# Splitting the weights of the head loops on ACT and DVE in a two-layer recurrent decoder step

## What is computed

```python
def _hgrn_mixer(h, w_in, lb, out_norm, w_out, S0):
    proj = h @ w_in
    q, fz, i, g = jnp.split(proj, [HGRN_F, 2 * HGRN_F, 2 * HGRN_F + D_MODEL], axis=-1)
    ...
    o, S = _hgrn_recurrence(q, k, v, log_f, S0.astype(F32))
    o = _rmsnorm(o, out_norm) * jax.nn.silu(g...)
    return o.reshape(B, T, D_MODEL).astype(h.dtype) @ w_out, S

def _trunk(x, ...):
    for i in range(DEPTH):
        h = _rmsnorm(x, norm_mix[i])
        y, S = _hgrn_mixer(h, ...) if i % N_MIXERS == 0 else _gdn_mixer(h, ...)
        x = x + y
        u = _rmsnorm(x, norm_mlp[i]) @ mlp_w_up[i]
        x = x + jnp.square(jax.nn.relu(u)) @ mlp_w_down[i]
```

## Time and profile before

| | |
|---|---|
| three runs | 2123.45, 2127.5, 2131.67 us; median 2127.5 us |
| span of the profiled execution (first to last instruction) | 2127.4 us |
| PE busy | 1885.8 us (89%) |
| DVE busy | 1200.8 us (56%) |
| POOL busy | 776.9 us (37%) |
| ACT busy | 449.8 us (21%) |
| mean granted clock of PE | 0.898 |

### The profile page before, as it was taken

One profiled execution on the slowest core, in us unless ns is written; L12 is line 12 of the kernel. 1 busy time (PEld: TensorE's weight loads), 2 busy tenths in 40 slices (PEclk: granted clock), 3 DMA queues, 4 the chain that ended last, 5 costly groups with the idle time before them and its releaser, 6 DMA issues.

```text
span 2127.4 us, 34241 instructions
## 1 busy us (share of the span) xinstructions
PE 1885.8 (89%) x13227; PEld 1784.2 (84%) x13227; DVE 1200.8 (56%) x1818; ACT 449.8 (21%) x899; POOL 776.9 (37%) x423
## 2 busy tenths in 40 slices
PE   4798888888999999996789889889878899999997
PEld 3788888887999999996678778778767899999996
DVE  5777777785744242575455555465561573516163
ACT  1323322331100000012233233233341110000011
POOL 1422222222566555563121211121210365656562
PEclk9988888888999999998789888888885999999998
DMA  5122221221233322231111211211100123322331
GB/s 161 50 61 60 60 59 52 60 61 42 83 87 90 90 78 84 79 81 52 40 31 43 52 30 41 52 30 41 52 21 21 55 86 90 89 82 87 89 89 42
DMA packets 257434, 135.99 MB, mean 64 GB/s; under 512 B 6698, under 2 KB 255876, under 8 KB 257348
## 3 DMA queue, kind: packets, MB, share of 16 engines
q1 hardware_dynamic: 219700, 114.03, 18.8%
q10 hardware_dynamic: 37648, 20.68, 3.3%
HBM read 122.70 MB, written 12.00 MB: 63 GB/s over the span
## 4 chain that ended last, share of the span: by engine, by line
PE 42%; DVE 6%; ACT 3%; issue 2%; POOL 0%; DVEq 0%; ACTq 0%; POOLq 0%
PE pj L449 27%; PE rr L487 2%; PE rr L699 2%; PE rr L723 2%; DVE pr L1532 1%; PE rr L470 1%; PE rr L715 1%; PE rr L792 1%; PE rr L708 1%; DVE ws L1603 1%; PE rr L780 1%; PE rr L644 1%; DVE ol L1742 1%; ACT ws L1028 1%; PE rr L798 1%
## 5 line engine op out<-in xcount | busy, mean ns | idle before, releaser
L416 POOL TENSOR_SCALAR w_hi<-w_raw 128x1024 fp32r<-128x1024 f32 x209 | 223.5, 1069 | 1299.5 <-PE pj L449 1268.8
L418 POOL TENSOR_TENSOR w_lo<-w_raw,w_hi 128x1024 fp32r<-128x1024 f32 x209 | 553.0, 2646 | 17.5
L449 PE MATMUL pj<-xh,w_hi 128*128 128x272 f32 x2064 | 480.2, 316 | 19.4 <-DVE xl L1298 10.0
L449 PE MATMUL pj<-xh,w_lo 128*128 128x272 f32 x2064 | 453.2, 303 | 0.0
L449 PE MATMUL pj<-xl,w_hi 128*128 128x272 f32 x2064 | 452.7, 303 | 0.0
L449 PEld LDWEIGHTS pj<-xh,w_hi 128*128 128x128 f32 x2064 | 348.9, 204 | 48.7 <-issue 30.2
L449 PEld LDWEIGHTS pj<-xl,w_hi 128*128 128x128 f32 x2064 | 350.9, 204 | 0.0
L449 PEld LDWEIGHTS pj<-xh,w_lo 128*128 128x128 f32 x2064 | 350.1, 204 | 0.0
L449 PE MATMUL pj<-oh,w_hi 128*128 128x272 f32 x1280 | 271.2, 293 | 16.7 <-DVE ol L1322 5.4
L449 PE MATMUL pj<-oh,w_lo 128*128 128x272 f32 x1280 | 268.3, 292 | 0.0
L449 PE MATMUL pj<-ol,w_hi 128*128 128x272 f32 x1280 | 267.2, 291 | 0.0
(11 more groups left out here) (275 smaller groups left out, 2290.0 us busy)
## 6 DMA issues: line engine op xcount, KB each, us to landing
w_raw<-in_mlp_w_up_dram SPq DMA_DIRECT2D x64, 512.0 KB, 4.0
w_raw<-in_mlp_w_down_dram SPq DMA_DIRECT2D x64, 512.0 KB, 3.7
w_raw<-in_hgrn_w_in_dram SPq DMA_DIRECT2D x32, 512.0 KB, 4.0
w_raw<-in_gdn_w_in_dram SPq DMA_DIRECT2D x32, 512.0 KB, 4.1
out_dram<-S ACTq DMA_DIRECT2D x16, 512.0 KB, 3.3
S<-in_state_hgrn_dram ACTq DMA_DIRECT2D x8, 512.0 KB, 4.0
w_raw<-in_hgrn_w_out_dram SPq DMA_DIRECT2D x8, 512.0 KB, 3.7
S<-in_state_gdn_dram ACTq DMA_DIRECT2D x8, 512.0 KB, 4.1
```

The lines of the kernel that those rows point to most:

```text
L416: nc.gpsimd.tensor_scalar(w_hi[:, s], w_raw[:, j], 1.0, 1.0, ALU.mult, ALU.mult).then_inc(w_split, 1)
L418: nc.gpsimd.tensor_tensor(w_lo[:, s], w_raw[:, j], w_hi[:, s], ALU.subtract).then_inc(w_split, 1)
L449: last = mm(pj[:, s, b, 0:HALF], w[:, s, k, :], v[:, k, b * HALF:(b + 1) * HALF], start=(k == 0 and a == 0), stop=(k == KT - 1 and a == 2))
```

## The change

Units 4 to U_HOUT + 1 and U_GIN + 4 to U_GOUT + 1, thirty in each layer, are no longer split by POOL. ACT makes the high part (`high`, an activation of kind Copy) and DVE the low part (`low`, a subtraction), at places written by hand into the programs of the heads. POOL keeps the first units of each layer and the MLPs. One semaphore becomes four, and whoever waits for a low part asks the semaphore of the engine that makes it (`low_part`). In SP's loads the first two heads and the output projections are unrolled, so that each knows its semaphore; the transfers and their order stay. In the diff below `run` (a loop over POOL's units) and the unrolled loads are left out.

```diff
-        w_split = sem("weights_split")
+        hi_act = sem("high_parts_by_scalar")
+        hi_pool = sem("high_parts_by_gpsimd")
+        lo_dve = sem("low_parts_by_vector")
+        lo_pool = sem("low_parts_by_gpsimd")
...
+        def on_gpsimd(u):
+
+            return u < 4 or U_HOUT + 2 <= u < U_GIN + 4 or u >= U_GOUT + 2
+
+        POOL_UNITS = [u for u in range(U_END) if on_gpsimd(u)]
+        DVE_UNITS = [u for u in range(U_END) if not on_gpsimd(u)]
+
+        def split_count(u):
+
+            part = POOL_UNITS if on_gpsimd(u) else DVE_UNITS
+            return part.index(u) + 1
+
+        def low_part(r, u):
+
+            at = r + u if isinstance(r, int) else u + (8 if u < U_HOUT - RAW or U_GIN - RAW <= u < U_GOUT - RAW else 0)
+            return (lo_pool if on_gpsimd(at) else lo_dve), split_count(at) - (at - u) + r
+
+        def raw_count(u):
+
+            return 16 * (u // RAW + 1) + (16 if u >= U_AB and u % RAW == U_AB % RAW else 0)
...
-                    free = fixed(sp, r * 2 + (2 * (U + j) - 6))
+                    done, n = low_part(r, U + j - RAW)
+                    free = fixed(sp, n)
                     sp.wait_ge(x_in[0], 16)
-                    sp.wait_ge(w_split, free)
+                    sp.wait_ge(done, free)
...
-            def split(n, j, extra=0):
-                u, s = n * 4 + j, j % SPLIT
-                loaded, free = fixed(pool, n * 16 + (16 + extra)), fixed(pool, u - 1)
+            def split(r, u):
+
+                j, s = u % RAW, u % SPLIT
+                at = r + u if isinstance(r, int) else u + 4
+                count = split_count(at) - (at - u) + r
+                loaded, free = fixed(pool, r * 4 + raw_count(at) - 4 * (at - u)), fixed(pool, r + u - 1)
+                written = fixed(pool, count)
                 pool.wait_ge(ones_set, 1)
                 pool.wait_ge(w_in[j], loaded)
-                if not (isinstance(n, int) and u < SPLIT):
+                if not (isinstance(r, int) and r + u < SPLIT):
                     pool.wait_ge(w_used, free)
-                nc.gpsimd.tensor_scalar(w_hi[:, s], w_raw[:, j], 1.0, 1.0, ALU.mult, ALU.mult).then_inc(w_split, 1)
-                pool.wait_ge(w_split, u * 2 + 1)
-                nc.gpsimd.tensor_tensor(w_lo[:, s], w_raw[:, j], w_hi[:, s], ALU.subtract).then_inc(w_split, 1)
-
-            for j in range(RAW):
-                split(0, j)
-            with pool.Fori(1, U_AB // 4) as n:
-                for j in range(RAW):
-                    split(n, j)
-
-            ab = U_AB % RAW
-            with pool.Fori(U_AB // 4, U_END // 4) as n:
-                for j in range(RAW):
-                    split(n, j, 16 if j == ab else 0)
-            for j in range(U_END % 4):
-                split(U_END // 4, j, 16 if j == ab else 0)
+                nc.gpsimd.tensor_scalar(w_hi[:, s], w_raw[:, j], 1.0, 1.0, ALU.mult, ALU.mult).then_inc(hi_pool, 1)
+                pool.wait_ge(hi_pool, written)
+                nc.gpsimd.tensor_tensor(w_lo[:, s], w_raw[:, j], w_hi[:, s], ALU.subtract).then_inc(lo_pool, 1)
...
+            for u in range(4):
+                split(0, u)
+            run(U_HOUT + 2, U_AB)
+            for u in range(U_AB, U_GIN + 4):
+                split(0, u)
+            run(U_GOUT + 2, U_END)
...
-                    pe.wait_ge(w_split, u * 2 + 2)
+                    pe.wait_ge(*low_part(r, U + j))
...
+            def high(h, u):
+
+                j, s = u % RAW, u % SPLIT
+                loaded, free = fixed(act, h * 16 + raw_count(u)), fixed(act, h * 4 + (u - 1))
+                act.wait_ge(w_in[j], loaded)
+                act.wait_ge(w_used, free)
+                f(w_hi[:, s], w_raw[:, j], ACT.Copy).then_inc(hi_act, 1)
...
                         hgrn_prepare(n, nxt)
+                        if m == 4:
+                            high(nxt, 2)
+                        if m == 32:
+                            high(nxt, 3)
                 if nxt is not None:
                     hgrn_prepare(7, nxt)
+                    high(nxt, 4)
...
                 s.did(f(oh[:, ds(h, 1)].rearrange("p o n -> p (o n)"), oo, ACT.Copy), "hi")
                 if nxt is not None:
+                    high(nxt, 5)
...
+            def gdn_head(h, prev, nxt, final=False):
 
                 v, s, t = st["gr"]
                 X, Tt, VN, oo, sqr = (gd[n] for n in ("X", "Tt", "VN", "oo", "sq"))
+                if nxt is not None:
+                    high(nxt, U_GIN + 3)
...
                         gdn_prepare(f"L{n}", nxt)
+                        if m == 16:
+                            high(nxt, U_GIN + 4)
...
                         gdn_prepare(f"C{c}", nxt)
+                        if c == 0:
+                            high(nxt, U_GIN + 5)
+                        if c == NC - 1 and not final:
+                            high(nxt, U_GIN + 6)
...
             for slot in range(3, 10):
                 hgrn_prepare(slot, 0)
+            high(0, 4)
+            high(0, 5)
...
                 gdn_prepare(slot, 0)
+            high(0, U_GIN + 4)
+            high(0, U_GIN + 5)
             gdn_first_inverse(0)
+            high(0, U_GIN + 6)
...
+            def low(h, u):
+
+                written = fixed(dve, h * 4 + (split_count(u + 4) - 4))
+                dve.wait_ge(hi_act, written)
+                tt(w_lo[:, u % SPLIT], w_raw[:, u % RAW], w_hi[:, u % SPLIT], ALU.subtract).then_inc(lo_dve, 1)
...
                         hgrn_prepare(n, nxt)
+                        if m == 8:
+                            low(nxt, 2)
+                        if m == 32:
+                            low(nxt, 3)
...
                     hgrn_prepare(8, nxt)
+                    low(nxt, 4)
                 out_tail(h, v, s, V_HON, hg["oo"], hg["sq"], hg["gate"], va)
                 if nxt is not None:
                     hgrn_prepare(9, nxt)
+                    low(nxt, 5)
...
                     gdn_prepare("L0", nxt)
+                    low(nxt, U_GIN + 3)
...
                         gdn_prepare(f"L{n}", nxt)
+                        if m == 32:
+                            low(nxt, U_GIN + 4)
...
                         gdn_prepare(f"C{c}", nxt)
+                        if c == 0:
+                            low(nxt, U_GIN + 5)
                 if nxt is not None:
                     gdn_prepare("inverse", nxt)
+                    if not final:
+                        low(nxt, U_GIN + 6)
...
             for slot in range(2, 10):
                 hgrn_prepare(slot, 0)
+            low(0, 4)
+            low(0, 5)
...
-            for slot in GDN_SLOTS + ["inverse", "move"]:
+            for slot in GDN_SLOTS + ["inverse"]:
                 gdn_prepare(slot, 0)
+            low(0, U_GIN + 4)
+            low(0, U_GIN + 5)
+            gdn_prepare("move", 0)
+            low(0, U_GIN + 6)
```

More of the change, by code:

```diff
@@ L364, in _ @@
             gin = gdn_w_in[0].rearrange("(k p) n -> p k n", p=P)
-            for j in range(4):
-                load(U_HIN, 0, j, hin[:, :, HGRN_ORDER[j] * D:HGRN_ORDER[j] * D + P])
-            with sp.Fori(1, H) as h:
+            for h in range(2):
+                for j in range(4):
+                    c0 = h * P + HGRN_ORDER[j] * D
+                    load(U_HIN, h * 4, j, hin[:, :, c0:c0 + P])
+            with sp.Fori(2, H) as h:
                 for j in range(4):
@@ L372, in out_proj @@
                 view = w[0].rearrange("(k p) n -> p k n", p=P)
-                with sp.Fori(0, 2) as i:
-                    for j in range(4):
-                        load(U, i * 4, j, view[:, :, ds(i * (4 * P) + j * P, P)])
+                for j in range(KT):
+                    load(U, 0, j, view[:, :, j * P:(j + 1) * P])
             def mlp(layer, U):
@@ L391, in _ @@
             slot = U_AB % RAW
-            sp.wait_ge(w_split, 2 * U_AB - 6)
+            sp.wait_ge(*low_part(0, U_AB - RAW))
             with nc.allow_non_contiguous_dma(reason="16 columns"):
@@ L396, in _ @@
                                  gin[:, :, 4 * D + n * H:4 * D + (n + 1) * H]).then_inc(w_in[slot], 16)
-            with sp.Fori(0, H) as h:
+            for h in range(2):
+                for j in range(4):
+                    c0 = h * P + GDN_ORDER[j] * D
+                    load(U_GIN, h * 4, j, gin[:, :, c0:c0 + P])
+            with sp.Fori(2, H) as h:
                 for j in range(4):
@@ new lines, in split, with run @@
+                pool.wait_ge(hi_pool, written)
+                nc.gpsimd.tensor_tensor(w_lo[:, s], w_raw[:, j], w_hi[:, s], ALU.subtract).then_inc(lo_pool, 1)
+            def run(first, end):
+                start = -(-first // RAW) * RAW
+                stop = end // RAW * RAW
+                for u in range(first, start):
+                    split(0, u)
+                with pool.Fori(0, (stop - start) // RAW) as n:
+                    for j in range(RAW):
+                        split(n * RAW, start + j)
+                for u in range(stop, end):
```

(7 more changed lines are left out.)

## The result

The changed kernel takes 2068.4 us (median of four runs, 2059.8 to 2075.1) against 2125.5 us (four runs of the kernel before beside them): a ratio of 0.972, 95% interval 0.969 to 0.975. Measured a second time beside other runs it came out at the same ratio, 0.972 (0.966 to 0.977). That is 57 us less where 32.5 were forecast. The profiled execution shown here has a span of 2057.6 us and is the fastest of its four, so between the two traces the gap is 69.8 us.

The account below looks back on a forecast made before the run. Waits in front of PE, many for DVE instructions standing still while POOL works, were taken to bound the recurrent stages. Savings 19 + 3.5 + 2 + 0 + 8 = 32.5 us from 2127.4 gave 2095; range 2066 to 2117.

Parts of the forecast that it names:

- what stood still, and why: DVE instructions L1415, L1462 and L1603 stand still while POOL works; without POOL's splits they fall to their minima.
- Not POOL: Rival: long DVE instructions aren't POOL's doing, stay, and 4.8 us a head come on top; inside the slower share, 0.07.
- the waits in the HGRN heads: PE's waits: 1.0 us less before the first level, 1.7 at unit 2; 2.7 us a head, 19 us over seven.
- The first head: Preparation of HGRN head 0: lengthened L1357 and L1361 go, so PE starts its tiles earlier; 3.5 us, bounds 0.3 to 3.6.
- the delta heads: Delta-rule heads: shorter waits against new ones, net gain 0.3 us a head, 2 us; first head's preparation taken as 0.
- PE's clock: HGRN heads: half of the half-clock stretch 220 to 226 us goes, 1.1 us a head, 8 us; delta layer nothing.
- More clock comes back: Rival: both half-clock places of HGRN heads vanish, as much in delta heads; up to 46 us instead of 8; chance 0.23.
- The clock gives nothing: Rival: PE's clock gains nothing, only 24.5 us come off, giving 2103 us; chance 0.20.
- No change: Rival: PE's two new waits come out twice as long, clock gives nothing; 2120 us (2117 to 2133); chance 0.08.
- Slower, by the clock: Rival: PE's clock falls behind each new or lengthened wait, two more 3-us stretches in 14 heads; 2134 us; chance 0.07.

## Why the prediction was right and where it was not

**Right: what stood still, and why.** The long DVE instructions are at their minima, and with POOL's useless subtractions they are long again. Rival *Not POOL* is out.

**Right: the waits in the HGRN heads.** Taken 2.7 us a head, 2.8 measured by the two bases. The wait for unit 2's low part is 0.93 us (1 said), the first level's is 2.68 (2.7 said), and the second has gone. The first head: PE reaches dS of head 0 at 97.0 us instead of 101.0, 4 us where 3.5 were taken; but 3.4 us at half clock went on the way there, some 1.5 us by the 0.446 above, so about 2.5 are left for the waits and the match is in part luck.

**Right in the single waits, wrong in the sum: the delta heads.** PE's wait before r1 rose to 2.24 (2.3 said) and that for r3 fell from 4.58 to 1.96 (2.4 said). The net 0.3 us a head is 0 by the bases. Up to the first dSs0 (preparation and head 0) the trace has 4.6 us less, with 11.8 us less at half clock, which is all of it by 0.43; 0 was taken, with bounds to 2.1 that left the clock out.

**Mis-sized: PE's clock, 8 us.** This is the step that failed. In the HGRN heads the two traces have 105.8 and 61.4 us at half clock; 44.4 x 0.446 is 20 us. With 7 x 2.8 = 19.6 that makes 39.4, and from the first to the last dS the traces differ by 39.9. In the delta heads 1 to 5 it is 51.1 us at half clock less, 22 of 23.3 us; head 6, which has no tiles to put into its chunks, got 4.8 us longer, with 11.6 us more at half clock. So the clock gave 20 us and, in this execution, about as much in the delta layer, where 8 and 0 stood; by the medians, with 57 us in place of 69.8, it gave less, some 35 (an estimate: 57 less the 22 of the HGRN waits). The step failed in three places. It kept the stretch behind the first wait and took half of the one behind the second, by the rule that a wait of 2.6 us has half clock behind it; the first was right (it even grew), but the second went whole or to 3.4 us. It left out the 3.2 us at 229.7, which are no wait's neighbour and went too, in all heads but one. And it set the delta layer to nothing, although the wait of 4.58 us stood ahead of 10 to 17 us at half clock; filling this wait alone reproduces the layer's gain. The price of 0.37 us for each us at half clock (1.1 for 3) was near the 0.446 measured.

**The rivals.** *More clock comes back* is what happened: 2075 halfway, 2057 at its limit, 2068 measured, and its reasons (the half-clock places follow the waits; the delta heads' longest wait falls) were the right ones. *The clock gives nothing* would be 2103. *No change* fails on its waits: 0.93 and 2.24 us, not twice what was summed. *Slower, by the clock* fails, though not everywhere on its condition. The new pause of 0.93 us has full clock around it (246.1 to 262 in one head), and so has that of 2.24 in the second delta head (1118 to 1132). But in two of the delta heads 1 to 5 half clock sets in at the end of that pause (1347.7 to 1351.1; the pause ends at 1347.9), and the clock falls behind the last pause of a delta head, 1.96 us (1132.7 to 1139.4). Already in the kernel before, a pause of 1.35 us has half clock behind it (a row of PE's timeline, then a stretch):

```profile
1160.36 0.40 PE L713 MATMUL rr<-ws 32*128 32x32 f32 x2 [1.35 <-ACT ws L1169]
...
1161.40:1168.20 6.80, 6.80 (x34) 6.22 (x33) 4.02 (x7) 1.98 (x4) 2.70 (x2) 0.50 0.00 0
```

So the length of a single pause does not decide. What the rival had wrong is the balance: over all heads the shortened waits took more half clock away than the new ones brought.

**The spread.** With one and the same delta program this part took 688 to 703 us (690.5 and 694.1 in the two profiles of the changed kernel itself), so some us of the gain belong to the execution and not to the kernel.

## What to carry to other kernels

Where a stage mixes long and short matmuls with waits, price a wait twice: its own length, and the half-clock time behind it (here 0.42 to 0.45 us for each us); read head length against half-clock time over many heads and the two come apart by themselves. Before moving work to free an engine, fill the suspected wait with useless matmuls: it costs a few lines and tells how much of the gain is the clock. Take two-input work off POOL before one-input work (here the subtractions before the copies), and put what is added where its engine has a pause, not where its consumer stands next.

## What was not expected of the hardware

Useless work made the kernel faster: 2.6 us of matmuls in one wait of six heads took 19 us off the run (2127.7 to 2109.0).

The same instructions take 45.8 or 50.3 us in neighbouring heads, and 73.2, 76.7 or 78.5 us in delta heads of one execution; only the granted clock differs.

The first MLP takes 10 to 13 us more in the kernels without useless matmuls in the HGRN heads (13 in the kernel before). At two of its group boundaries PE stands for 1.9 us and again for 1.95, here in the kernel before:

```profile
750.04 0.51 PE L449 MATMUL pj<-xh,w_hi 128*128 128x272 f32 x2 [1.94 <-POOL w_hi L416]
752.99 0.61 PE L449 MATMUL pj<-xh,w_hi 128*128 128x272 f32 x2 [1.95 <-issue]
```

With the fillers, which lengthen PE's program of the HGRN heads, both pauses and the half clock behind them are gone. "Issue" means that nothing which the profile shows was waited for. The cause wasn't tried and stays open; the second MLP, with the same instructions, has no such pause in any kernel.
